# Three planes of expert three's gate and up matrices loaded ahead of the expert loop, and g_final loaded behind it

## The chip, the cores and the metric

One NeuronCore of a Trainium2 chip runs the whole kernel in one launch. The metric is the device time of one execution in microseconds (us). The engines of the core are PE (matmuls), DVE (vector), ACT (scalar), POOL and SP; SP computes nothing here and only issues loads. All transfers run on the core's 16 DMA engines.

## The reference

One step of a one-layer encoder: 512 prompt tokens and 32 sample tokens of width 1024. Two attention branches, merged by gates, then a mixture of experts, then a per-layer embedding gate and a last norm. The expert part is what matters here:

```
h = rmsnorm(x, g_ffn)
group = argmax(h @ w_group + b_group)                       # 4 groups of 8 experts
two experts of that group by top_k(softmax(h @ w_router))   # weights: softmax of both
for each block of rows of an expert e (32 experts):
    out = (silu(rows @ w_gate[e]) * (rows @ w_up[e])) @ w_down[e]    # 1024 -> 512 -> 1024
x = x + weighted sum of each token's two rows
x = x + sigmoid(rmsnorm(x, g_ple) @ w_ple_gate) * (p @ w_ple)
y = rmsnorm(x, g_final)
```

All is float32. An expert's three matrices are 2 MB each, 6 MB together, and all 32 experts are read once.

## The kernel before, in words

The front part (attention, merge, output projection) runs on PE until about 450 us. Then the rows are normed, stored to a DRAM tensor `normed_rows` (by ACT, semaphore `xn_stored` for the four prompt tiles), routed, and a table of rows for each expert is made on PE and DVE. Every expert has a block of 64 rows; an expert with more gets extra blocks after the loop. The 32 experts are worked off in 16 pairs. For a pair POOL gathers 128 rows by an indirect DMA (`xs_in`, three places), PE transposes them, DVE scales them (`xsT`); then for each of the two experts PE makes the gate and up products (`gate_up`, semaphore `gu_done`), ACT the silu, DVE the product, PE transposes it and makes the down product (`down`, `dn_done`), ACT copies the result out and POOL scatters it to a DRAM tensor `expert_rows` (`ye_stored`).

SBUF has places for the gate and up matrices of three experts (`w_gu[0..2]`, 32 KB in each partition, `gu_in[k]`), and four for down matrices. A matrix 1024 x 512 lies as 8 planes of 512 columns in each partition. `load_gu(k, e)` loads both matrices of expert `e` into place `k`; `load_planes(e, n, lo, hi)` loads planes `lo` to `hi` of one matrix, n = 0 for gate, 1 for up. Expert 3 uses place 0 again, after expert 0.

All weight loads are issued by SP, in the order in which they are written, on one hardware queue; SP's waits are what holds a load back. The order before the loop: expert 0 whole; the down matrix of expert 2; two quarters of expert 3's down matrix (`load_dn_over_rows`, each over a tile of rows that is done with); planes of expert 2; a third quarter; the down matrix of expert 1 and its gate planes; the first four planes of its up matrix; then, behind the wait for the first gather of rows (`xs_in[0]`, line 674), what is left of experts 1 and 2. From expert 3 on each gate and up load waits until PE has finished the same products of the expert three before (`next_gate_up` waits for `gu_done` at `e - 2`), and each down load until `dn_done` is at `e - 2`.

Behind the loop SP loads the inputs of the embedding gate, half of `w_ple_gate`, and `x_nat` from `normed_rows`; then it waits for the last expert and for all scatters (`ye_stored`), and loads for each tile the expert rows of its tokens (`yg`, in the order 0, 4, 1, 2, 3), with the other half of `w_ple_gate` behind the second.

The constants (router weights and biases, `g_fin`, sinks, gains) are loaded near the start on the semaphore `consts_in`; their readers wait for `16 * CONSTS`, lines 829, 1682 and 2055. `g_fin` holds `g_final` in all partitions, 4 KB in each. It is read in the last norms (`finish`) and by `keep_busy`, PE's filler matmuls at about 459 to 466 us, whose result nobody reads. Router tiles (`rt_...`) lie at 65 to 69.25 KB of the arena; `at(kb, dims)` gives the place at `kb` KB. The exponentials of the router are ACT's, released by `rt_exp_in`.

Of the kernel before, what the change touches and what calls it, by code (L numbers as in the profile page):

```python
# [32 lines left out]
P = 128  # L33
D = 1024
KD = D // P
# [22 lines left out]
GROUPS, PER = 4, 8  # L58
# [17 lines left out]
assert BODIES * BODY == PAIRS - 1 and 2 * BODY % PLACES == 0  # L76
CONSTS = 8
SLICES = 4
# [150 lines left out]
def _program(nc, A, ctx):  # L229
# [158 lines left out]

    work, keep = (65, 69.25), (130.25, 131.25)
    x_turned = [hb[:, 4 * D:5 * D].rearrange("p (c t) -> p c t", c=KD), xf[:, 4, :].rearrange("p (c t) -> p c t", c=KD),  # L390
# [11 lines left out]
    place_hot = rt(work, [2, 2, BLK])  # L402
    rt_thr, rt_step, rt_cnt = rt(work, [PER]), rt(work, [OVER]), rt(work, [EXPERTS])
    rt_cmp = rt(work, [EXPERTS, PER])
    rt_over = rt(work, [1])
    picks = at(69.25, [TILES, EXPERTS], BF16)
# [3 lines left out]
    w_dn = [[at(114.25, [4, D])], [hb[:, 0:4 * D].rearrange("p (c n) -> p c n", c=4)], [at(70.5, [2, D]), at(131.25, [2, D])]]  # L410
    w_dn.append([x_nat[:, c:c + 1, :] for c in range(4)])

    def dn_place(e):
# [140 lines left out]
    def _(sp):  # L554
# [28 lines left out]
        load(b_rt[:, GROUPS:], A['b_router'].to_broadcast([P, EXPERTS]), consts_in)  # L583
        load(g_fin[:, :], A['g_final'].unsqueeze(0).to_broadcast([P, D]), consts_in)
        load(sink_in[:, :], A['attn_sink'].to_broadcast([P, HEADS]), consts_in)
# [73 lines left out]
        load_dn_over_rows(0)  # L659
        load_dn_over_rows(1)  # L660
        sp.wait_ge(rows_full, 4)
        load_planes(2, 0, 0, 2)
# [9 lines left out]
        load_planes(1, 1, 2, 4)  # L672
        sp.wait_ge(rows_full, TILES)
        sp.wait_ge(xs_in[0], 16)
        load_planes(2, 1, 5, 8)
        load_planes(1, 1, 4, 6)
        load_planes(1, 1, 6, 8)
        for c in range(2, KD, 2):
            load_planes(2, 0, c, c + 2)
        load_planes(2, 1, 0, 1)  # L680
        load_planes(2, 1, 3, 5)
        load_dn_over_rows(3)

        def next_gate_up(k, e):
# [9 lines left out]
        LOOP = 2 * BODY  # L694
        for e in range(PLACES, PLACES + LOOP):
            next_gate_up(e % PLACES, e)
            if e > PLACES:
                next_down(dn_place(e), e)
        with sp.Fori(0, BODIES - 2) as i:
# [24 lines left out]
        sp.wait_ge(xn_stored, 16 * 4)  # L724
        load(x_nat[:, 0:4, :], xn_d[0:NP].rearrange("(t p) n -> p t n", p=P), x_in[0])

        sp.wait_ge(dn_done, EXPERTS)
# [195 lines left out]
    def _(pe):  # L923
# [427 lines left out]
        def keep_busy(n):  # L1351
            for _ in range(n):
                pe.matmul(ps[:, 2, :], ident[:, :], g_fin[:, 0:512], start=True, stop=True)

# [4 lines left out]
        def rows_turned(k, lo=0, hi=KD):  # L1359
# [4 lines left out]
            return mm  # L1364

        def expert_columns(k, m, c, g):

            return w_gu[k][:, m, c, :].rearrange("p m (q g j) -> p m q g j", g=2, j=2)[:, :, :, g, :]

        def gate_up(s, k, col):  # L1370
            for c in range(KD):
                for g in range(2):
                    mm = pe.matmul(ps[g * BLK:(g + 1) * BLK, 2 + s, :], xsT[:, c, col:col + BLK],  # L1373
                                   expert_columns(k, slice(0, 2), c, g), start=c == 0, stop=c == KD - 1)
            return mm
# [26 lines left out]
        def pair(i, body, j):  # L1402

            p = i * BODY + (body * BODY + j)
            for s in range(2):
                e = 2 * (body * BODY + j) + s
                k, use, d = e % PLACES, i * (2 * BODY // PLACES) + (e // PLACES + 1), dn_place(e)
                if s == 0:
                    pe.wait_ge(xsT_ready, p + 1)
                pe.wait_ge(gu_in[k], use * 32 + (32 * SLICES - 32 if k else 0))  # L1410
                gate_up(s, k, s * BLK).then_inc(gu_done, 1)
                if s == 0:
                    pe.wait_ge(xs_in[(j + 1) % 3], i * 16 + 16 * ((body * BODY + j + 1) // 3 + 1))
                    rows_turned((j + 1) % 3).then_inc(xsT_full, 1)
                pe.wait_ge(hid_ready, p * 2 + (s + 1))
                turn_hidden(s).then_inc(hidT_full, 1)
                pe.wait_ge(hidT_ready, p * 2 + (s + 1))
                pe.wait_ge(dn_in[d], i * (2 * BODY // PLACES * 16 * len(w_dn[d])) + dn_use(e) * 16 * len(w_dn[d]))
                pe.wait_ge(ye_free, p * 2 + (s + 1))
                down(s, d).then_inc(dn_done, 1)  # L1420
# [14 lines left out]
        half_of_expert(k, 0, 0, 1, 0).then_inc(gate_done, 1)  # L1435
        pe.wait_ge(gu_in[k], use * 32 + (32 * SLICES - 32 if k else 0) - 16)
        half_of_expert(k, 0, 1, 2, 256).then_inc(gu_done, 1)
# [10 lines left out]
        half_of_expert(k, 1, 0, 0, 0).then_inc(gate_done, 1)  # L1448
        pe.wait_ge(gu_in[k], use * 32 + (32 * SLICES - 32 if k else 0) - 16)
        half_of_expert(k, 1, 1, 3, 256).then_inc(gu_done, 1)  # L1450
# [493 lines left out]
    def _(dve):  # L1944
# [566 lines left out]
        def finish(i):  # L2511
            t = LAST_ORDER[i]
            r = ROWS[t]
            dve.wait_ge(x4_squares, i + 1)
            v = rstd(r, i)
# [63 lines left out]
```

## Time and profile before

| | us |
|---|---|
| median of three executions | 1022.1 (1021.7 to 1022.69) |
| the profiled execution | 1020.0 |
| its span, first to last instruction | 1017.9 |
| mean granted TensorE clock | 0.98 |
| PE busy | 911.9 (90%) |
| TensorE weight loads busy | 585.0 (57%) |
| DVE, ACT, POOL busy | 379.0, 258.3, 141.3 |
| chain that ended last: PE, DMA, DVE | 61%, 29%, 4% |
| of it, the load of up matrices | 26% |
| read from HBM, written | 256.09 MB, 16.85 MB |

The chain of waits is followed back from the last instruction: at each step to what released it, or to the instruction before it on its engine. A time to landing is that from the issue of a DMA until its semaphore has the last of 16 increments. All times below are microseconds from the span's start. "SPq" marks SP's instruction queue; L556 is the helper through which SP issues every load.

### The profile page before, as it was taken

The page shows a single profiled execution, that of the slowest core. Times are in us where ns is not written, and L with a number is a line of the kernel's source. Part 1 is how long each engine was busy: PE and PEld are TensorE (multiplying, and loading weights), DVE is VectorE, ACT ScalarE, POOL GpSimd, SP SyncE. Part 2 cuts the span into 40 slices and gives each one's busy share as a digit, 9 for nine tenths or more (in the row PEclk, how much of TensorE's full clock was granted, in tenths as well). Part 3 has the DMA queues.
Part 4 walks back from the last instruction along what each step waited for, and adds up shares of the span by engine and source line. Part 5 has one row for each costly group of instructions (what it writes and reads, how often), then busy time and mean ns, then how long its engine had stood idle before and what let it go on. Part 6 is the DMA issues. An engine that isn't in the chain of part 4 may idle for free.

```text
span 1017.9 us, 14245 instructions
## 1 busy us (share of the span) xinstructions
PE 911.9 (90%) x5747; PEld 585.0 (57%) x5750; DVE 379.0 (37%) x973; ACT 258.3 (25%) x525; POOL 141.3 (14%) x146
## 2 busy tenths in 40 slices
PE   7999999989999999989999988788887787888996
PEld 7969995557999997973333322222232222334775
DVE  4279998754233354362111110100110101113696
ACT  6354328664231342231000000000000000002542
POOL 2705432122110000001111101001101011000000
PEclk9999999999999999998999999999999999999998
DMA  8860602005734406487999999999999999997601
GB/s 268 115 162 1 208 1 63 1 2 164 220 77 110 119 2 269 150 311 298 423 423 428 426 429 425 426 427 426 427 425 427 426 427 427 428 422 317 259 22 68
DMA packets 61096, 265.88 MB, mean 261 GB/s; under 512 B 11118, under 2 KB 36094, under 8 KB 47312
## 3 DMA queue, kind: packets, MB, share of 16 engines
q1 hardware_dynamic: 55120, 253.08, 65.1%
q0 software_dynamic: 5296, 9.79, 2.7%
q10 hardware_dynamic: 624, 2.23, 0.6%
q8 instruction: 39, 0.64, 0.3%
q14 instruction: 17, 0.14, 0.0%
HBM read 256.09 MB, written 16.85 MB: 268 GB/s over the span
## 4 chain that ended last, share of the span: by engine, by line
PE 61%; DMA 29%; DVE 4%; issue 3%; ACT 2%; SPq 1%; POOL 0%; DVEq 0%; POOLq 0%; ACTq 0%
DMA arena<-in_w_up 26%; PE ps L1205 14%; PE ps L1373 12%; PE ps L1060 5%; PE ps L1238 4%; PE ps L1526 4%; PE ps L1398 4%; PE ps L1006 3%; PE ps L981 2%; PE ps L1150 2%; PE ps L1129 1%; PE ps L1099 1%; PE ps L943 1%; PE ps L1267 1%; PE ps L936 1%
## 5 line engine op out<-in xcount | busy, mean ns | idle before, releaser
L1373 PE MATMUL ps<-arena,hT 128*64 128x512 f32 x960 | 231.7, 635 | 37.9 <-DMA arena<-in_w_up 37.8
L1373 PEld LDWEIGHTS ps<-arena,hT 128*64 128x64 f32 x960 | 70.1, 139 | 196.6 <-issue 146.9
L2342 DVE TENSOR_TENSOR xf<-xf,ps 128x256 f32<-128x256 f32 x32 | 13.5, 421 | 398.1 <-ACT xf L1819 375.5
L1205 PE MATMUL ps<-arena_merge,arena_merge 128*128 128x256 f32 x624 | 99.7, 287 | 0.0
L891 POOL DMA_INDIRECT expert_rows<-xf,arena x32 | 32.0, 1001 | 422.9 <-ACT xf L1823 396.9
L1398 PE MATMUL ps<-arena,xf 128*64 128x512 f32 x336 | 76.7, 597 | 14.8 <-DVE xf L2345 13.4
L1205 PEld LDWEIGHTS ps<-arena_merge,arena_merge 128*128 128x128 f32 x624 | 87.5, 188 | 0.0
L1205 PE MATMUL ps<-xf_merge,arena_merge 128*128 128x256 f32 x480 | 82.0, 288 | 0.0
L1819 ACT ACTIVATE xf<-ps 128x256 f32<-128x256 f32 x30 | 11.5, 384 | 255.0 <-PE ps L1373 255.0
L1205 PEld LDWEIGHTS ps<-xf_merge,arena_merge 128*128 128x128 f32 x480 | 69.3, 188 | 0.0
L1823 ACT ACTIVATE xf<-ps 128x512 f32<-128x512 f32 x30 | 17.9, 597 | 160.9 <-PE ps L1398 160.9
L1398 PEld LDWEIGHTS ps<-arena,xf 128*64 128x64 f32 x336 | 25.7, 136 | 51.3 <-issue 48.5
L1238 PE MATMUL ps<-arena_merge,arena_merge 128*128 128x256 f32 x304 | 49.0, 286 | 1.2 <-DVE arena_merge L2176 1.0
L1526 PE MATMUL ps<-arena_gate,arena_gate 128*128 128x512 f32 x192 | 44.3, 391 | 1.3 <-DVE arena_gate L2484 0.8
L1238 PEld LDWEIGHTS ps<-arena_merge,arena_merge 128*128 128x128 f32 x304 | 42.9, 191 | 2.5 <-DVE arena_merge L2176 2.0
L2176 DVE TENSOR_TENSOR arena_merge<-arena,arena_merge 128x256 fp32r<-128x256 f32 (+2 forms) x34 | 39.9, 1226 | 9.0 <-ACT arena_merge L1590 9.0
L1060 PE MATMUL ps<-xf_merge,arena_front 128*128 128x272 f32 x256 | 43.2, 289 | 0.0
L1590 ACT ACTIVATE arena_merge<-arena 128x256 fp32r<-128x256 f32 (+3 forms) x43 | 37.1, 919 | 21.3 <-DMA arena<-in_w_branch_a 10.4
L1398 PE MATMUL ps<-hT,xf 128*64 128x512 f32 x160 | 36.5, 598 | 5.2 <-DVE xf L2345 5.2
L1526 PEld LDWEIGHTS ps<-arena_gate,arena_gate 128*128 128x128 f32 x192 | 35.8, 188 | 9.2 <-ACT arena L1861 1.0
L1060 PEld LDWEIGHTS ps<-xf_merge,arena_front 128*128 128x128 f32 x256 | 36.2, 189 | 0.2
L1687 ACT ACTIVATE arena<-arena,stat 128x257 f32<-128x257 f32 (+7 forms) x57 | 29.6, 520 | 4.0 <-DVE stat L2094 4.0
(323 smaller groups left out, 1306.2 us busy)
## 6 DMA issues: line engine op xcount, KB each, us to landing
arena<-in_w_gate SPq DMA_DIRECT2D x30, 2048.0 KB, 30.5
arena<-in_w_up SPq DMA_DIRECT2D x30, 2048.0 KB, 37.3
arena<-in_w_down SPq DMA_DIRECT2D x11, 2048.0 KB, 36.0
arena<-in_w_down SPq DMA_DIRECT2D x20, 1024.0 KB, 30.9
hT<-in_w_down SPq DMA_DIRECT2D x10, 2048.0 KB, 36.5
arena<-in_w_in SPq DMA_DIRECT2D x10, 1024.0 KB, 6.5
arena<-in_w_in SPq DMA_DIRECT2D x3, 2048.0 KB, 11.1
arena<-in_w_gate SPq DMA_DIRECT2D x8, 512.0 KB, 9.0
```

Source lines behind the costliest of these rows:

```text
L891: pool.indirect_dma_start(ys, bass.IndirectOffsetOnAxis(ap=of, axis=0), src, None, bounds_check=row_bound, oob_is_err=False).then_inc(s, 16)
L981: mm = pe.matmul(w[:, a * 512:a * 512 + HALF], rounded(st, "front"), rounded(mv[:, c, a * HALF:(a + 1) * HALF]), start=c == 0 and k == 0, ...
L1006: mm = pe.matmul(ps[0:ROWS[t], 6 + slot, 0:256], rounded(st[:, c, tok(t)]), rounded(mv[:, c, :], "front"), start=c == 0 and k == 0, stop=c ...
L1060: mm = pe.matmul(w[:, a * 512:a * 512 + HALF], rounded(st, "front"), rounded(mv[:, c, a * HALF:(a + 1) * HALF]), start=c == 0 and k == 0, ...
L1205: mm = pe.matmul(w[:, 2 * lo_t:lo_t + hi_t], rounded(st[:, c, cols]), rounded(mv[:, c, lo_t:hi_t]), start=c == 0 and k == 0, stop=c == pla ...
L1238: mm = pe.matmul(w[:, q * QW:(q + 1) * QW], rounded(st[t // 2][:, t % 2, m, :]), rounded(mv[:, m, :]), start=m == 0 and k == 0, stop=m == ...
L1373: mm = pe.matmul(ps[g * BLK:(g + 1) * BLK, 2 + s, :], xsT[:, c, col:col + BLK], expert_columns(k, slice(0, 2), c, g), start=c == 0, stop=c ...
L1398: mm = pe.matmul(ps[g * BLK:(g + 1) * BLK, 6 + s, :], hidT[s][:, c % 2, c // 2 * BLK:(c // 2 + 1) * BLK], dn_at(k, c)[:, g * 512:(g + 1) * ...
L1526: mm = pe.matmul(w[:, cols], rounded(st[:, c, :], "gate"), rounded(mv[:, c, cols], "gate"), start=c == 0 and k == 0, stop=c == KD - 1 and ...
L1590: return act.activation(rounded(dst, stage), src, ACT.Copy)
L1687: act.activation(v, v, ACT.Exp, bias=stat[:, 0, g, j:j + 1], scale=-1.0, accum_out=stat[:, 1, g, j:j + 1]).then_inc(exp_done, 1)
L2176: return dve.tensor_tensor(rounded(v, stage), v, rounded(hi, stage).bitcast(F32), ALU.subtract)
```

## The change

The matrices of expert 3 are loaded in two parts. Planes 0, 1 and 2 of its gate and up matrices get rooms of their own, 4 KB in each partition: room 0 is the tile `g_fin`, room 1 lies at 64.5 to 68.5 KB of the arena, room 2 in two pieces at 68.5 and at 112 KB. Room 0 is loaded behind the second quarter of expert 3's down matrix, rooms 1 and 2 behind the fourth quarter and a wait for `rt_exp_in`. All six loads count on `gu_in[0]`, and a wait for expert 0's two loads stands ahead of the first. Planes 3 to 7 are loaded, as before, when PE has finished expert 0's products. PE reads the rooms in the first pass of the loop's first body alone, for expert 3; every wait on `gu_in[0]` from expert 3 on is higher by 96.

Three loads of 512 KB, planes 4 to 7 of expert 1's up matrix and planes 2 and 3 of expert 2's gate matrix, move from behind the wait for the first gather to ahead of it, behind a new wait for `xn_stored`.

`g_fin` is loaded behind `x_nat` near the end, as `CONSTS` is now 7, and DVE waits for it before the first `finish`. `keep_busy` reads the identity matrix four times over in its place. Some router tiles move to 78.5 to 80 KB.

```diff
--- before.py
+++ after.py
@@ -74,7 +74,7 @@
 BODY = 3
 BODIES = (PAIRS - 1) // BODY
 assert BODIES * BODY == PAIRS - 1 and 2 * BODY % PLACES == 0
-CONSTS = 8
+CONSTS = 7
 SLICES = 4
 
 
@@ -386,7 +386,7 @@
         assert rt_at[lo] <= int(hi * 256)
         return at(first / 256, dims, dt)
 
-    work, keep = (65, 69.25), (130.25, 131.25)
+    work, keep, late = (65, 69.25), (130.25, 131.25), (78.5, 80)
     x_turned = [hb[:, 4 * D:5 * D].rearrange("p (c t) -> p c t", c=KD), xf[:, 4, :].rearrange("p (c t) -> p c t", c=KD),
                 at(78.5, [KD, NS])]
     turned_in = {0: x_turned[0], 1: x_turned[0], 2: x_turned[1], 3: x_turned[0], 4: x_turned[2]}
@@ -400,15 +400,27 @@
     rt_el, rt_t1, rt_t2 = rt(work, [EXPERTS + 8]), rt(work, [EXPERTS + 8]), rt(work, [EXPERTS + 8])
     rt_free, rt_pen = rt(work, [8 + GROUPS]), rt(work, [GROUPS])
     place_hot = rt(work, [2, 2, BLK])
-    rt_thr, rt_step, rt_cnt = rt(work, [PER]), rt(work, [OVER]), rt(work, [EXPERTS])
-    rt_cmp = rt(work, [EXPERTS, PER])
-    rt_over = rt(work, [1])
+    rt_cmp = rt(late, [EXPERTS, PER])
+    rt_thr, rt_step, rt_cnt = rt(late, [PER]), rt(late, [OVER]), rt(late, [EXPERTS])
+    rt_over = rt(late, [1])
     picks = at(69.25, [TILES, EXPERTS], BF16)
     rt_ti = at(69.75, [EXPERTS]).bitcast(I32)
 
     w_gu = [at(32.5, [2, KD, DE]), at(0, [2, KD, DE]), at(80, [2, KD, DE])]
     w_dn = [[at(114.25, [4, D])], [hb[:, 0:4 * D].rearrange("p (c n) -> p c n", c=4)], [at(70.5, [2, D]), at(131.25, [2, D])]]
     w_dn.append([x_nat[:, c:c + 1, :] for c in range(4)])
+
+    def apart(kb, step):
+
+        v = at(kb, [DE])
+        return bass.AP(tensor=v.tensor, offset=v.offset, ap=[v.ap[0], [int(step * 256), 2], [1, DE]])
+
+    ROOMS = [g_fin[:, :].rearrange("p (m n) -> p m n", m=2), at(64.5, [2, DE]), apart(68.5, 112 - 68.5)]
+    ROOM_LOADS = 2 * len(ROOMS)
+
+    def gu_count(e, k, use):
+
+        return use * 32 + (32 * SLICES - 32 if k else 16 * ROOM_LOADS if e >= PLACES else 0)
 
     def dn_place(e):
 
@@ -581,7 +593,6 @@
         load(w_rt[:, :, GROUPS:], A['w_router'][0].rearrange("(p c) n -> p c n", c=KD), consts_in)
         load(b_rt[:, 0:GROUPS], A['b_group'].to_broadcast([P, GROUPS]), consts_in)
         load(b_rt[:, GROUPS:], A['b_router'].to_broadcast([P, EXPERTS]), consts_in)
-        load(g_fin[:, :], A['g_final'].unsqueeze(0).to_broadcast([P, D]), consts_in)
         load(sink_in[:, :], A['attn_sink'].to_broadcast([P, HEADS]), consts_in)
         load_gain(1, consts_in)
         load_gain(2, consts_in)
@@ -658,6 +669,14 @@
 
         load_dn_over_rows(0)
         load_dn_over_rows(1)
+
+        def load_room(c):
+
+            for m in range(2):
+                load(ROOMS[c][:, m], A[('w_gate', 'w_up')[m]][0, PLACES].rearrange("(p c) n -> p c n", c=KD)[:, c], gu_in[0])
+
+        sp.wait_ge(gu_in[0], 32)
+        load_room(0)
         sp.wait_ge(rows_full, 4)
         load_planes(2, 0, 0, 2)
         load_planes(2, 1, 1, 3)
@@ -671,15 +690,20 @@
         load_planes(1, 1, 0, 2)
         load_planes(1, 1, 2, 4)
         sp.wait_ge(rows_full, TILES)
+        sp.wait_ge(xn_stored, 16 * 4)
+        load_planes(1, 1, 4, 6)
+        load_planes(1, 1, 6, 8)
+        load_planes(2, 0, 2, 4)
         sp.wait_ge(xs_in[0], 16)
         load_planes(2, 1, 5, 8)
-        load_planes(1, 1, 4, 6)
-        load_planes(1, 1, 6, 8)
-        for c in range(2, KD, 2):
+        for c in range(4, KD, 2):
             load_planes(2, 0, c, c + 2)
         load_planes(2, 1, 0, 1)
         load_planes(2, 1, 3, 5)
         load_dn_over_rows(3)
+        sp.wait_ge(rt_exp_in, 1)
+        load_room(1)
+        load_room(2)
 
         def next_gate_up(k, e):
 
@@ -692,10 +716,13 @@
             load_dn(k, e)
 
         LOOP = 2 * BODY
-        for e in range(PLACES, PLACES + LOOP):
+        sp.wait_ge(gu_done, 1)
+        for m in range(2):
+            load(w_gu[0][:, m, len(ROOMS):], A[('w_gate', 'w_up')[m]][0, PLACES].rearrange(
+                "(p c) n -> p c n", c=KD)[:, len(ROOMS):], gu_in[0])
+        for e in range(PLACES + 1, PLACES + LOOP):
             next_gate_up(e % PLACES, e)
-            if e > PLACES:
-                next_down(dn_place(e), e)
+            next_down(dn_place(e), e)
         with sp.Fori(0, BODIES - 2) as i:
             for e in range(PLACES + LOOP, PLACES + 2 * LOOP):
                 next_gate_up(e % PLACES, i * LOOP + e)
@@ -723,6 +750,7 @@
         load(w_pg[:, 0:KD // 2], w_pg_d[:, 0:KD // 2], w_pg_in[0])
         sp.wait_ge(xn_stored, 16 * 4)
         load(x_nat[:, 0:4, :], xn_d[0:NP].rearrange("(t p) n -> p t n", p=P), x_in[0])
+        load(g_fin[:, :], A['g_final'].unsqueeze(0).to_broadcast([P, D]), consts_in)
 
         sp.wait_ge(dn_done, EXPERTS)
         sp.wait_ge(slots_ready, 1)
@@ -1350,7 +1378,7 @@
 
         def keep_busy(n):
             for _ in range(n):
-                pe.matmul(ps[:, 2, :], ident[:, :], g_fin[:, 0:512], start=True, stop=True)
+                pe.matmul(ps[:, 2, :], ident[:, :], ident[:, :].unsqueeze(1).to_broadcast([P, 4, P]), start=True, stop=True)
 
         keep_busy(3)
         pe.wait_ge(index_ready, 3)
@@ -1363,15 +1391,20 @@
                 mm = pe.transpose(w[:, c, :], xs[k][:, c:D:KD], ident[:, :])
             return mm
 
+        def every_other(w, g):
+
+            return w.rearrange("p m (q g j) -> p m q g j", g=2, j=2)[:, :, :, g, :]
+
         def expert_columns(k, m, c, g):
 
-            return w_gu[k][:, m, c, :].rearrange("p m (q g j) -> p m q g j", g=2, j=2)[:, :, :, g, :]
-
-        def gate_up(s, k, col):
+            return every_other(w_gu[k][:, m, c, :], g)
+
+        def gate_up(s, k, col, rooms=[]):
             for c in range(KD):
                 for g in range(2):
                     mm = pe.matmul(ps[g * BLK:(g + 1) * BLK, 2 + s, :], xsT[:, c, col:col + BLK],
-                                   expert_columns(k, slice(0, 2), c, g), start=c == 0, stop=c == KD - 1)
+                                   every_other(rooms[c], g) if c < len(rooms) else expert_columns(k, slice(0, 2), c, g),
+                                   start=c == 0, stop=c == KD - 1)
             return mm
 
         def half_of_expert(k, s, m, bank, col):
@@ -1407,8 +1440,8 @@
                 k, use, d = e % PLACES, i * (2 * BODY // PLACES) + (e // PLACES + 1), dn_place(e)
                 if s == 0:
                     pe.wait_ge(xsT_ready, p + 1)
-                pe.wait_ge(gu_in[k], use * 32 + (32 * SLICES - 32 if k else 0))
-                gate_up(s, k, s * BLK).then_inc(gu_done, 1)
+                pe.wait_ge(gu_in[k], gu_count(e, k, use))
+                gate_up(s, k, s * BLK, ROOMS if body == 0 and e == PLACES else []).then_inc(gu_done, 1)
                 if s == 0:
                     pe.wait_ge(xs_in[(j + 1) % 3], i * 16 + 16 * ((body * BODY + j + 1) // 3 + 1))
                     rows_turned((j + 1) % 3).then_inc(xsT_full, 1)
@@ -1433,7 +1466,7 @@
         pe.wait_ge(xsT_ready, p + 1)
         pe.wait_ge(gate_in[0], 16)
         half_of_expert(k, 0, 0, 1, 0).then_inc(gate_done, 1)
-        pe.wait_ge(gu_in[k], use * 32 + (32 * SLICES - 32 if k else 0) - 16)
+        pe.wait_ge(gu_in[k], gu_count(EXPERTS - 2, k, use) - 16)
         half_of_expert(k, 0, 1, 2, 256).then_inc(gu_done, 1)
         pe.wait_ge(hid_ready, p * 2 + 1)
         turn_hidden(0).then_inc(hidT_full, 1)
@@ -1446,7 +1479,7 @@
         k, use = (EXPERTS - 1) % PLACES, (EXPERTS - 1) // PLACES + 1
         pe.wait_ge(gate_in[1], 16)
         half_of_expert(k, 1, 0, 0, 0).then_inc(gate_done, 1)
-        pe.wait_ge(gu_in[k], use * 32 + (32 * SLICES - 32 if k else 0) - 16)
+        pe.wait_ge(gu_in[k], gu_count(EXPERTS - 1, k, use) - 16)
         half_of_expert(k, 1, 1, 3, 256).then_inc(gu_done, 1)
         pe.wait_ge(rows_in, 32 + 32)
         for c in range(2):
@@ -2511,6 +2544,8 @@
         def finish(i):
             t = LAST_ORDER[i]
             r = ROWS[t]
+            if i == 0:
+                dve.wait_ge(consts_in, 16 * (CONSTS + 1))
             dve.wait_ge(x4_squares, i + 1)
             v = rstd(r, i)
             dve.scalar_tensor_tensor(yo[t][0:r, :], x_nat[0:r, t, :], v, g_fin[0:r, :], ALU.mult, ALU.mult)\
```

## Rows read from the trace of the kernel before

**Rows 1.** The page, second part: busy tenths in 40 slices of the span.
```profile
DMA  8860602005734406487999999999999999997601
```

**Rows 2.** Stretches: length, each engine's busy us (instructions), PE clock, DMA share, GB/s.
```profile
core 0: us, PE busy (x) PEld busy (x) DVE busy (x) ACT busy (x) POOL busy (x), PEclk, DMA share, GB/s
456.60:462.00 5.40, 4.32 (x18) 2.46 (x19) 3.38 (x20) 1.60 (x3) 1.46 (x2) 0.50 0.01 5
...
490.00:580.00 90.00, 83.17 (x384) 30.56 (x382) 9.55 (x18) 6.87 (x14) 11.11 (x11) 1.00 1.01 425
580.00:900.00 320.00, 259.79 (x1124) 89.78 (x1122) 28.23 (x50) 20.23 (x41) 30.22 (x30) 0.97 1.01 427
...
936.00:942.00 6.00, 5.46 (x24) 4.50 (x25) 3.41 (x3) 3.10 (x3) 0.52 (x1) 1.00 0.27 105
```

**Rows 3.** Waits of PE, 460 to 920 us: total us, times, longest us.
```profile
PE ps L1373 <- DMA arena<-in_w_up: 37.8, 20, 3.3
```

**Rows 4.** The chain of waits, whole span: start, us, what.
```profile
460.24 4.52 DMA xf<-normed_rows,arena
464.89 0.69 PE ps L1363 x4
465.61 1.30 DVE hT L2374 x2
466.95 7.42 PE ps L1373 x32
...
577.90 35.69 DMA arena<-in_w_up
```

**Rows 5.** Timeline of SP's issues: start, us, instruction.
```profile
474.42 0.33 SPq L556 DMA_DIRECT2D arena<-in_w_gate  x1
474.79 0.43 SPq L556 DMA_DIRECT2D arena<-in_w_up  x1
487.24 0.33 SPq L556 DMA_DIRECT2D arena<-in_w_gate  x1
487.61 0.43 SPq L556 DMA_DIRECT2D arena<-in_w_up  x1
...
500.05 0.33 SPq L556 DMA_DIRECT2D arena<-in_w_gate  x1
```

**Rows 6.** DMA issues, the one at 474.79: size, us to landing.
```profile
arena<-in_w_up SPq DMA_DIRECT2D x1, 2048.0 KB, 16.7
```

**Rows 7.** ACT's store of the last rows: timeline, and DMA issues.
```profile
454.28 0.33 ACTq L1780 DMA_DIRECT2D normed_rows<-xf  x1
...
normed_rows<-xf ACTq DMA_DIRECT2D x1, 512.0 KB, 3.6
```

**Rows 8.** SP's issues at 382 us, queue empty, and their us to landing.
```profile
382.27 0.35 SPq L556 DMA_DIRECT2D arena<-in_w_gate  x1
382.67 0.43 SPq L556 DMA_DIRECT2D arena<-in_w_up  x1
...
arena<-in_w_gate SPq DMA_DIRECT2D x1, 2048.0 KB, 8.3
...
arena<-in_w_up SPq DMA_DIRECT2D x1, 2048.0 KB, 12.8
```

**Rows 9.** Stretches around room 0's issue, columns as in rows 2.
```profile
426.00:431.00 5.00, 5.00 (x44) 5.00 (x44) 1.30 (x9) 1.02 (x1) 0.00 (x0) 1.00 0.25 69
436.00:438.00 2.00, 2.00 (x19) 2.00 (x19) 1.79 (x14) 1.22 (x2) 0.00 (x0) 1.00 0.07 23
```

**Rows 10.** DMA issues, the one at 487.61: size, us to landing.
```profile
arena<-in_w_up SPq DMA_DIRECT2D x1, 2048.0 KB, 14.4
```

**Rows 11.** DMA issues, a 512 KB load at 429.01: us to landing.
```profile
x_nat<-in_w_down SPq DMA_DIRECT2D x1, 512.0 KB, 3.8
```

**Rows 12.** POOL's gather of rows issued at 495.04: us to landing.
```profile
DMA to landing us min/median/max: 13.5/13.5/13.5
```

**Rows 13.** DMA issues, `g_fin` at 24.64: us to landing.
```profile
g_fin<-in_g_final SPq DMA_DIRECT2D x1, 512.0 KB, 3.7
```

**Rows 14.** SP's issue of `x_nat`: timeline, and us to landing.
```profile
917.74 3.11 SPq L556 DMA_DIRECT2D x_nat<-normed_rows  x1
...
x_nat<-normed_rows SPq DMA_DIRECT2D x1, 2048.0 KB, 25.5
```

**Rows 15.** The chain of waits behind the loop: start, us, what.
```profile
941.31 5.18 DMA arena<-expert_rows
946.59 1.30 DVE x_nat L2466
```

## The prediction

> **What bounds the kernel now.** I read the page's DMA line first [rows 1]: from the twentieth of 40 slices (about 483 us) to the thirty-sixth the 16 DMA engines are full. The stretches say it more sharply [rows 2]: between 456.6 and 462 us they are idle (share 0.01), between 490 and 580 us full at 425 GB/s, between 580 and 900 us full at 427 GB/s. PE's waits in the expert loop are nearly all for a weight load, 37.8 us in 20 waits [rows 3]. In the chain [rows 4] a load is first the late step at 577.90 us: up to there PE sets the pace (one expert in some 12.8 us), from there on the DMA stream does. The reader is to take from this that the end follows the time at which this unbroken stream gets through its bytes, and that bytes moved out of it count only if the stream can then really run earlier.
>
> What lets it run is the queue's own waits [rows 5]. The loads of expert 3 go out at 474.42, of expert 4 at 487.24, of expert 5 at 500.05: each as PE has finished the gate and up products of the expert that held the place (`gu_done`). That is PE's clock, not the DMA's. So the question of this change is how late the stream is when expert 4's loads are issued. Expert 3's up matrix, issued at 474.79, lands 16.7 us later, 491.5 [rows 6]: 4.3 us after the issue of expert 4's. This is all the backlog there is at that moment.
>
> **The change part by part.**
>
> *Bytes taken out of the stream.* (a) Three loads of 512 KB (planes 4 to 7 of expert one's up, 2 and 3 of expert two's gate) move from behind the wait for the first gather to behind `xn_stored`. The last store of rows is issued at 454.28 and lands 3.6 us later, 457.9 [rows 7], so they run in the idle gap. (b) Room 0 of expert three, 512 KB, goes out behind the load at 429.01; its wait for `gu_in[0]` was over when expert zero's up landed, 382.67 + 12.8 = 395.5 [rows 8], so nothing is held up behind it. The DMAs are a quarter busy from 426 to 431 and nearly idle from 436 to 438 [rows 9], so its 1.2 us (524 KB at 425 GB/s) are hidden; were that cover gone it would push the loads behind it 1.2 us, and those have until 466 us. (c) Rooms 1 and 2, 1024 KB, are only moved ahead of 474.42, into a time when the stream is full in any case: nothing. The four extra issues on SP at some 0.4 us each are done by about 472, before SP's next wait ends at 474.42 [rows 5]: nothing. Together 2048 KB leave the stream ahead of expert 4. One such load lands behind the other 382.67 + 12.8 less 382.27 + 8.3, 4.9 us [rows 8].
>
> *How much of it counts.* With 4.9 us less in front, expert 3's last piece would land at 491.5 - 4.9 = 486.6, ahead of the issue at 487.24, which no edit moves forward. The queue runs dry and has to start again from empty. What that costs is in the trace: at 382.67 an up matrix was issued behind a gate matrix with the queue empty, as expert 4's would be now, and landed after 12.8 us [rows 8]. So expert 4's up would land at 487.61 + 12.8 = 500.4; before it landed at 487.61 + 14.4 = 502.0 [rows 10]. The gain is 1.6 us, not 4.9. Bounds: 4.3 (all of the backlog, if the start from empty cost nothing) and 0 (if the DMA engine that is last at 900 us is one that had caught up at 487 us already; the spread of the engines is not in a view). I take 1.6, from the row that has the same two loads in the same order. From 490 us on the queue never empties again, and this gain lasts to the end of the stream.
>
> Beside that row stands a rule of the Trainium skill, "DMA: Bandwidth & Descriptors", section "Anatomy of one DMA": a fixed cost of about 2.0 us and bytes at 436 GB/s. The trace has 8.3 less 4.9, 3.4 us, for a 2048 KB load from empty. By the rule the up matrix would land at 498.9 and the step would be worth an estimated 3 us; the row decides the sum, and the rule's result is the second rival below.
>
> *The gather's delay.* The three loads share the DMAs with the first gather of rows, which is on the chain: issued at 460.24, landed 4.52 us later, then PE's transposes, DVE, and expert 0 at 466.95 [rows 4]. In the trace of before nothing else runs there. A 512 KB load issued on a quiet queue lands after 3.8 us [rows 11]; two more and the gather itself, 524 KB each at 425 GB/s, make 457.9 + 3.8 + 3.7 = 465.4 for the last of the four, 0.6 us behind the 464.8 of before. Everything PE does shifts by this, the issue of expert 4's loads too, so it is lost in full. Bounds: 0 (the gather gets through between the loads) and 9.0, since a gather in the full loop takes 13.5 us and not 4.5 [rows 12]. I take 0.6: at 460.24 the queue holds three short loads, no loop of them.
>
> *The tail.* `g_fin`, 512 KB, leaves the constants at 24.64 us, where nothing on the chain waits for it (it took 3.7 us there [rows 13]; PE is busy with projections), so taking it out is worth nothing: its first reader is the last norm. It comes back behind the load of `x_nat`, which is issued at 917.74 and lands 25.5 us later, 943.2 [rows 14]. That is later than the issue of the first gathered output rows at 941.31 on the same queue, and those are on the chain: they land 5.18 us on, and DVE starts at 946.59 [rows 15]. So at least one DMA engine now has 1.2 us more before it can turn to them. On the average the DMAs are only 0.27 busy between 936 and 942 us [rows 2], so the other engines swallow it. Bounds 0 and 1.2; I take 0.9, nearer to the slowest engine, because a landing is that of the last of the 16. The wait for `g_fin` on DVE itself costs nothing: it stands before the first norm of an output, more than 30 us after that load.
>
> *Nothing else.* PE's clock filler reads the identity matrix in place of `g_fin`, 512 columns as before, in a time when PE waits for the gather. The moved router tiles change addresses, no instruction. The gate and up products of expert 3 read three planes from other places, same shapes, and those are there 30 us ahead.
>
> Sum: -1.6 + 0.6 + 0.9 = -0.1 us on the profiled execution's 1020.0 us (span 1017.9, and 2.1 us around it): 1019.9. The median of the runs shown is 1022.1, 2.1 us above that execution; the same difference on it gives 1022.0.
>
> **The rivals.**
>
> *The prefetch counts for more.* If the stream is not dry at 487.24, or restarts at once, the step is worth up to the whole backlog, 4.3 us: -4.3 + 0.6 + 0.9 = -2.8, 1019.3. For it: the engines end at different times, and the last one may carry work across. Against it: 4.9 us are taken from a backlog of 4.3, and the row from empty. By the skill's fixed cost (section named above) it would be an estimated -1.5, 1020.6.
>
> *The gather waits behind weights (slower).* Place: 457.9 to 465 us. If the packets of the gather come behind those of the three loads as they do in the loop, its landing moves by up to 9.0 us and PE's whole schedule with it: the DMAs then simply stay dry for longer, as every later issue hangs on PE. Price at that bound: -1.6 + 9.0 + 0.9 = +8.3, 1030.4. It turns the result slower, by over 2 us, from a delay of 2.7 us on. For it: 13.5 against 4.5 us [rows 4, 12]. Against it: the loads hold 1536 KB, 3.7 us of work, of which over half is done when the gather's first packets could come.
> Here the Trainium skill, "DMA: Bandwidth & Descriptors", section "Queues, rings and completion order", speaks against the change: each DMA engine takes turns between its queue rows a whole packet at a time. By it the gather waits out a started packet at every turn, which no row of this gap shows; it is what would lead to this rival's delay, and its price is that from the rows above.
>
> *The prefetch is worth nothing.* The engine that ends last had no backlog at 487 us: 0 + 0.6 + 0.9 = +1.5, 1023.6.
>
> **How the numbers follow.** A difference of 0.2% (2 us) is about what a measurement tells from none. Forecast (-0.1, between -1.6 and +1.6 as the parts of it vary): 0.64. Nothing gained: 0.07. Both are within 0.2%, 0.71. The prefetch for more: 0.16, faster. The gather behind weights: 0.13, slower. The range reaches down to the first rival's 1019.3 and up to 1024.6, the last rival's 1023.6 with 1 us more of delay; most of the slow rival's long tail is left out.
>
> **What would show it.** DMA share above 0.5 between 459 and 462 us; the first gather's landing at 465.4 and expert 0's products at 467.5 in place of 466.95; between 485 and 489.5 us a dip in the DMA share that was not there; PE's first wait for a load a little later than at 577.9; the last down matrix about 1 us earlier; between 935 and 947 us some of it given back, with the first output rows landing 6 us after their issue. The prediction is wrong if there is no dip at 487 us, if the gather takes over 7 us, or if the end moves by more than 2 us either way.

## The result, and the profile after

The changed kernel takes 1024.86 us (median of 20 executions, 1022.65 to 1028.72), the kernel before 1021.78 (20 executions, 1019.68 to 1024.16): ratio 1.0029, 95% interval 1.0021 to 1.0037, slower by 3 us. The prediction was 1022.0, with a range from 1019.3 to 1024.6 and a chance of 0.13 for slower. Three single executions further below took 1810, 3115 and 5000 us and are left out of the ratios.

The profiled execution has a span of 1022.4 us against 1017.9, 4.5 us more. Where it arises can be read off the chain of waits (start, us, what), compared step by step with [rows 4, 15]:

```profile
462.31 5.20 DMA xf<-normed_rows,arena
467.64 0.70 PE ps L1391 x4
...
469.71 7.42 PE ps L1405 x32
...
580.65 35.88 DMA arena<-in_w_up
...
938.24 5.95 DMA expert_rows<-xf,arena
944.26 6.75 DMA arena<-expert_rows
951.11 1.30 DVE x_nat L2499
```

The gather is issued 2.07 us later (462.31 for 460.24) and takes 5.20 for 4.52; expert 0's products start at 469.71 for 466.95, 2.76 later. The output rows' load is issued at 944.26 for 941.31, 2.95 later, and takes 6.75 for 5.18, so DVE starts 4.52 later, which is the end's shift. So there are three large steps and a small one: 2.07 ahead of the gather, 0.68 in it, 0.2 over the whole loop, 1.57 in the tail.

The first is in code that the change hardly touches. In the stretches (length, busy us and instructions of each engine, PE clock, DMA share, GB/s) the changed kernel has PE at 1.2 GHz for 3.4 us where before had 2.4 GHz throughout (granted clock 0.57 and 1.00); the first fence is the changed kernel, the second the kernel before:

```profile
386.00:390.00 4.00, 3.95 (x19) 3.75 (x20) 2.66 (x3) 0.34 (x1) 0.00 (x0) 0.57 1.01 430
```
```profile
386.00:390.00 4.00, 3.92 (x30) 3.73 (x31) 2.85 (x3) 0.52 (x1) 0.00 (x0) 1.00 0.99 418
```

19 matmuls in 4 us and not 30: the rest of that work comes some 1.5 us later (an estimate: 11 matmuls at 4/30 us each). From 382 to 386 us PE is busy for 2.88 us in the changed kernel and for 2.90 in the one before, so what it did ahead of the stretch does not tell the two apart. Nor does the program decide it: e5 below is the changed kernel once more, and its profile has no such stretch. What is left of the 2.07 us has no cause in these views.

What the stream of weights does at expert 4's issue:

```profile
477.18 0.33 SPq L568 DMA_DIRECT2D arena<-in_w_gate  x1
477.55 0.43 SPq L568 DMA_DIRECT2D arena<-in_w_up  x1
490.00 0.33 SPq L568 DMA_DIRECT2D arena<-in_w_gate  x1
490.37 0.43 SPq L568 DMA_DIRECT2D arena<-in_w_up  x1
```
```profile
484.00:487.00 3.00, 3.00 (x16) 0.90 (x14) 0.00 (x0) 0.00 (x0) 1.04 (x1) 1.00 0.97 401
487.00:490.00 3.00, 2.95 (x14) 0.69 (x10) 0.00 (x0) 0.00 (x0) 0.00 (x0) 1.00 0.21 83
490.00:492.00 2.00, 0.59 (x4) 0.40 (x6) 0.99 (x3) 0.38 (x1) 0.00 (x0) 1.00 0.72 131
492.00:580.00 88.00, 81.69 (x373) 29.22 (x373) 9.46 (x16) 6.48 (x13) 11.13 (x11) 1.00 1.00 425
580.00:900.00 320.00, 260.61 (x1124) 92.65 (x1124) 29.05 (x52) 20.59 (x42) 30.23 (x30) 0.96 1.01 427
```
```profile
arena<-in_w_up SPq DMA_DIRECT2D x1, 2048.0 KB, 13.2
```

The timeline of SP, the stretches, and the time to landing of the up matrix issued at 490.37. The queue runs dry: the DMA share is 0.21 between 487 and 490, where before had 1.05. The matrix lands 13.2 us after its issue and not 14.4 [rows 10]; so at this point the stream is 1.2 us nearer to PE than before, where 12.8 and so 1.6 had been forecast. From 492 us on the DMA share and the rate are those of before [rows 2], and of the 1.2 us nothing is left at the end of the loop.

### The profile page after: what moved, and what is told of

It reads as the page before. It is cut to its first block, busy times and chain, and to the rows that moved or that the text cites. A ratio compares the mean times of both kernels' runs of the same rounds, so it can differ in the third digit from the quotient of the medians.

```text
span 1022.4 us, 14251 instructions
## 1 busy us (share of the span) xinstructions
PE 915.9 (90%) x5750; PEld 589.2 (58%) x5750; DVE 378.7 (37%) x973; ACT 258.2 (25%) x525; POOL 141.3 (14%) x146
## 4 chain that ended last, share of the span: by engine, by line
PE 60%; DMA 29%; DVE 5%; issue 3%; ACT 2%; SPq 0%; POOL 0%; DVEq 0%; POOLq 0%; ACTq 0%
DMA arena<-in_w_up 26%; PE ps L1233 13%; PE ps L1405 12%; PE ps L1088 5%; PE ps L1266 5%; PE ps L1559 4%; PE ps L1431 4%; PE ps L1034 3%; PE ps L1009 2%; PE ps L1178 2%; PE ps L1157 1%; PE ps L1127 1%; PE ps L1295 1%; PE ps L971 1%; PE ps L964 1%
## 5 line engine op out<-in xcount | busy, mean ns | idle before, releaser
L832 POOL TENSOR_TENSOR arena_front<-arena,arena_front 128x512 fp32r<-128x512 f32 (+1 forms) x17 | 24.8, 1491 | 42.6 <-ACT arena_front L1623 42.4
```

Source lines behind the costliest of these rows:

```text
L832: return pool.tensor_tensor(rounded(v, stage), v, rounded(hi, stage).bitcast(F32), ALU.subtract)
```

## The experiments

Theory A, formed on the two traces: the prefetched bytes bring nothing, since each of the 16 DMA engines starts expert 4 from empty, and the one that ends the loop last was one with no backlog before; the gather's delay and `g_fin`'s load are both paid in full; the rest is chance. Rival B: something that I had put at nothing (moved router tiles, the filler, the clock) costs 1 to 2 us, and the prefetch's 1.2 us are real.

The first four kernels are compared with the same runs of before, the next four with a second set, the last three with a third. The ratio stated can differ from that of the medians by up to 0.1%, and with some ten runs of a kernel its interval is some 0.1% wide to either side, about 1 us.

**e1, `g_fin` late alone.** On the kernel before:
```diff
-CONSTS = 8
+CONSTS = 7
-        load(g_fin[:, :], ..., consts_in)            # among the constants
         load(x_nat[:, 0:4, :], xn_d[0:NP]..., x_in[0])
+        load(g_fin[:, :], ..., consts_in)
# and the filler on ident, the wait in finish, as in the change
```


> The kernel before with only g_fin's load moved behind x_nat (and the filler reading the identity). Theory A (the tail pays for g_fin on the DMA engine that is last): the first output rows land some 6.7 us after their issue and not 5.2, the whole is slower by 1.2 to 1.8 us, ratio 1.0012 to 1.0018. Rival B (the quiet DMAs swallow it, the 4.5 us between the profiles came from earlier): within 0.5 us of before, 5.2 us to landing.

Measured: 1023.46 against 1022.03, ratio 1.0014 (1.0005 to 1.0023), 1.4 us slower. Its chain has the longer landing, 6.38 us for 5.18 [rows 15], a little less than the 6.7 expected:
```profile
937.69 6.01 DMA expert_rows<-xf,arena
943.78 6.38 DMA arena<-expert_rows
```
The tail's step stands alone; B's "swallowed" is out.

**e2, the three loads early alone.** On the kernel before:
```diff
         sp.wait_ge(rows_full, TILES)
+        sp.wait_ge(xn_stored, 16 * 4)
+        load_planes(1, 1, 4, 6); load_planes(1, 1, 6, 8); load_planes(2, 0, 2, 4)
         sp.wait_ge(xs_in[0], 16)
         load_planes(2, 1, 5, 8)
-        load_planes(1, 1, 4, 6); load_planes(1, 1, 6, 8)
-        for c in range(2, KD, 2):
+        for c in range(4, KD, 2):
```


> The kernel before with only the three 512 KB loads moved ahead of the wait for the first gather. Theory A (the stream runs dry at expert 4's issue and starts from empty for every DMA engine, so nothing of the 3.7 us is kept, and the gather's delay is lost in full): first gather 5.1 to 5.3 us to landing, slower by 0.5 to 1 us. Rival B (1.2 us of the prefetch last to the end): faster by about 0.5 us. Either way the up matrix of expert 4 lands 12.8 to 13.3 us after its issue, not 14.4.

Measured: 1023.09 against 1022.03, ratio 1.0011 (0.9999 to 1.0023). The interval touches 1, so the time alone leaves slower just short of shown; a gain of 0.5 us is outside it. Chain and stretches:
```profile
461.69 5.16 DMA xf<-normed_rows,arena
```
```profile
456.60:462.00 5.40, 2.96 (x16) 1.98 (x17) 4.12 (x27) 1.09 (x4) 0.31 (x1) 0.50 0.56 189
...
487.00:490.00 3.00, 2.31 (x12) 0.44 (x8) 0.23 (x1) 0.38 (x1) 0.00 (x0) 1.00 0.59 236
```
The gap of [rows 2] is filled (0.56 for 0.01), the gather pays 0.6 us for it, and the hole turns up again at 487 us (0.59). The up matrix of expert 4 lands 13.2 us after its issue, as expected.

**e3, the change with `g_fin` loaded later.**
```diff
         load(x_nat[:, 0:4, :], xn_d[0:NP]..., x_in[0])
-        load(g_fin[:, :], ..., consts_in)
         ...
                 load(w_pg[:, KD // 2:], w_pg_d[:, KD // 2:], w_pg_in[1])
+                load(g_fin[:, :], ..., consts_in)
```


> The changed kernel with g_fin loaded behind the first three loads of output rows' queue (behind the second half of w_ple_gate) and not ahead of them. Theory A: the first output rows land 5.2 us after their issue again, 1.2 to 1.8 us faster than the changed kernel, so before +1.3 to +1.8. Rival B (the tail is not the cause): still +3, though the landing may be 5.2.

Measured: 1022.73 against 1022.03, ratio 1.0006 (0.9995 to 1.0017). The changed kernel's ratio was 1.0029 and 1.0030 (e5): some 2.4 us come back, more than forecast, though the intervals leave room for the forecast 1.2 to 1.8. The first output rows land after 5.74 us, better than the change's 6.75 but not the 5.2 expected. The span of this profile, 1022.1, is hardly below the change's 1022.4, as PE's clock fell ahead of expert 0 here (see e7).

**e4, the rooms alone.** e3 with the three loads back behind `xs_in[0]`.

> As e3, and the three 512 KB loads back behind the wait for the first gather: only the three rooms are left. Theory A (prefetched planes of expert 3 are worth nothing, the rest of the change costs nothing): same as before within 0.5 us, first gather 4.5 us to landing. Rival B (the change costs something else, in the router tiles or in the clock around 386 us): still slower by 1 to 2 us. Rival C (the planes are worth their bytes): 1 to 2 us faster.

Measured: 1022.38 against 1022.03, ratio 0.9999 (0.9987 to 1.0011): no difference, with some 1.2 us of doubt to either side. Of the rooms only room 0, 512 KB or 1.2 us, leaves the stream here; it brings nothing, and the moved router tiles, the filler on the identity and the higher counts cost nothing that shows. The interval alone leaves B and C of that expectation their lower edges, 1 us; the loop of its profile is 0.1 us shorter than before (table below), which speaks against C.

**e5, the changed kernel again.**

> The changed kernel itself, run again beside the others. Theory A: 2.2 to 3 us slower than before (0.7 of the gather and 1.4 of g_fin's load, nothing gained), and the half clock stretch at 386 us that its first profile had and the profile of before had not is chance: this profile may well be without it, with the first gather issued at about 461 us. Rival B (the change causes that clock stretch): it is there again.

Measured: 1024.95 against 1021.74, ratio 1.003 (1.0017 to 1.0044). Stretch of its profile, same columns:
```profile
386.00:390.00 4.00, 3.90 (x30) 3.49 (x30) 3.10 (x4) 0.78 (x1) 0.00 (x0) 1.00 1.03 434
```
The same program, and no stretch at half clock at 386 us, so the change does not bring it about by itself. Two more of the later profiles have it (e7, e10), none of the three of kernels without rooms; whether the change makes it more frequent is not settled.

**e6, bytes added.** e4 with expert 3 loaded whole, and the rooms loaded late and unused:
```diff
-        sp.wait_ge(gu_in[0], 32)
-        load_room(0)                                  # the early one
         sp.wait_ge(rt_exp_in, 1)
+        load_room(0)
         load_room(1); load_room(2)                    # all on a semaphore room_in
-        # planes 3 to 7 of expert 3
+        next_gate_up(0, PLACES)                       # expert 3 whole
```


> As e4, but expert 3 is loaded whole and the three rooms (1536 KB, 3.7 us of DMA) are loaded late, behind the other loads, and read by nobody: bytes added ahead of expert 4 instead of taken out. Theory A (the DMA engine that ends last is just short of dry when expert 4's loads are issued, so bytes more cost all and bytes less bring nothing): 3 to 3.7 us slower than before. Rival B (this stretch has slack either way): within 1 us. Rival C (bytes count both ways, the gain was lost elsewhere): 3.7 us slower as well, and then e4 must have lost 1.2 us somewhere.

Measured: 1025.26 against 1021.74, ratio 1.0036 (1.0023 to 1.0049): 3.5 to 3.7 us slower for 3.7 us of DMA. Its up matrix of expert 4, issued at 487.06, lands 18.8 us later, for 14.4 before:
```profile
arena<-in_w_up SPq DMA_DIRECT2D x1, 2048.0 KB, 18.8
```
Bytes more at this place cost at least what they take (the loop of its profile is even 4.8 us longer), bytes less (e4, e2) bring nothing: the kernel before stood at the edge where its queue just fails to run dry.

**e7, the rooms for expert 4.** On e3. Expert 4's loads are the first that PE holds back at a dry queue; its planes leave the stream behind that point.
```diff
-   load(ROOMS[c][:, m], ...[0, PLACES]...[:, c], gu_in[0])
+   load(ROOMS[c][:, m], ...[0, PLACES + 1]...[:, c], room_in)
-        sp.wait_ge(gu_done, 1)                        # planes 3 to 7 of expert 3
+        next_gate_up(0, PLACES)                       # expert 3 whole
+        sp.wait_ge(gu_done, 2)                        # planes 3 to 7 of expert 4
# PE reads the rooms at e == PLACES + 1, behind a wait for room_in
```


> The rooms are given to expert 4 in place of expert 3 (own semaphore; expert 3 loaded whole; g_fin as in e3; the three 512 KB loads early). Bytes now leave the stream behind the issue of expert 4's loads. Theory A: 3.7 us less to load behind it, some 1.3 us of it lost as the queue is nearly dry at that issue, 0.7 lost by the gather: 1.5 to 3 us faster than before. Rival B (planes held in rooms are worth nothing wherever they belong): 0.5 to 1 us slower, as e3.

Measured: 1021.35 against 1021.74, ratio 0.9988 (0.9975 to 1.0002). The interval touches 1; B, slower by 0.5 to 1 us, is outside it, but the gain is smaller than forecast. The stretches of this kernel:
```profile
487.00:490.00 3.00, 3.00 (x16) 0.96 (x14) 0.00 (x0) 0.00 (x0) 0.00 (x0) 1.00 0.97 382
490.00:493.00 3.00, 2.06 (x10) 0.59 (x6) 0.42 (x1) 0.38 (x1) 0.00 (x0) 1.00 0.67 214
```
and PE's timeline:
```profile
461.20 4.78 PE L1383 MATMUL ps<-ident 128*128 128x512 f32 x6
467.91 1.46 PE L1393 MATMUL ps<-ident,xf 128*128 128x128 f32 x8 [1.94 <-DMA xf<-normed_rows,arena]
469.16 1.92 PE L1383 MATMUL ps<-ident 128*128 128x512 f32 x2
471.01 7.88 PE L1407 MATMUL ps<-arena,hT 128*64 128x512 f32 x32
```
The queue is short again at expert 4's issue (0.67 from 490 to 493 us). That costs nothing that shows: from expert 0's first product to the last scatter this kernel takes 465.5 us, and e9 below, whose queue is not short, 465.4. What is lost lies ahead of expert 0. The gather takes 5.41 us, and PE, idle for 1.94 us ahead of its landing, does the filler behind it at half clock (1.92 us for the 1.02 of most profiles), so expert 0 starts 3.2 us behind the landing (471.01 less 467.78), before 2.2 us [rows 4]. The profile of e3 has the same, 3.6 us. These two are among the five profiles with all three loads early; of the other eight none has it.

**e8, as e7 with the three loads back behind the gather.**

> As e7 with the three 512 KB loads back behind the wait for the first gather. Theory A: the stream ahead of expert 4 is 2.5 us longer, behind it 3.7 us shorter, nothing lost by the gather: 1 to 1.5 us faster than before. Rival B: the same as before.

Measured: 1020.43 against 1021.74, ratio 0.9979 (0.9967 to 0.9991). Faster, by 1.3 us in the medians and 2.1 by the ratio; rival B of e8 is out, and with e9 that of e7.

**e9 and e10, two loads early, and one.** On e8; the other stay behind the gather.
```diff
+        sp.wait_ge(xn_stored, 16 * 4)
+        load_planes(1, 1, 4, 6)
+        load_planes(1, 1, 6, 8)                       # e9 alone
         sp.wait_ge(xs_in[0], 16)
```


> As e8 (rooms for expert 4, g_fin last) with two of the three 512 KB loads ahead of the first gather: the stream ahead of expert 4's issue is as long as before, behind it 3.7 us shorter. Theory A: 3 to 3.5 us faster than before, less 0.2 to 0.5 for the gather. Rival B (each early load costs the gather its own time, whatever the number): as e8, 1.3 to 2 us faster.

> As e9 with one load early. Theory A: the stream ahead is 1.2 us longer, the gather is not touched: 2 to 2.5 us faster than before. Rival B: no faster than e8.

Measured: e9 1018.62, ratio 0.9964 (0.9951 to 0.9977); e10 1019.4, ratio 0.9973 (0.9963 to 0.9983), both against 1021.99. e9 has the lowest median of this study, 3.4 us below before (3.7 by the ratio, 2.3 to 5.0 by the interval) and some 6 below the change, from eight executions between 1016.3 and 1022.0. Its lead over e10 is within the intervals. The queue is not short around expert 4's issue at 492 us (share 1.06 from 490 to 493, 1.00 from 490 to 498), and the gather keeps nearly its time (4.52 before, 5.20 in the change):
```profile
490.00:493.00 3.00, 2.06 (x10) 0.57 (x6) 0.42 (x1) 0.39 (x1) 0.00 (x0) 1.00 1.06 450
```
```profile
464.56 4.76 DMA xf<-normed_rows,arena
...
936.95 5.95 DMA expert_rows<-xf,arena
942.97 5.45 DMA arena<-expert_rows
```

**e11, a fourth filler.** e9 with `keep_busy(4)`.

> As e9 with four filler matmuls ahead of the gather's landing and not three. Profiles with a late gather had PE idle for 1.7 to 2.4 us before the transposes, and two of them then a stretch at half clock over expert 0. Theory A (idle time, and so the half clock, is filled): 0 to 0.5 us faster than e9, no half clock stretch begins between 465 and 472 us. Rival B (the filler itself becomes late at half clock): 0.3 to 0.6 us slower than e9.

Measured: 1018.95 against 1021.99, ratio 0.9973 (0.9961 to 0.9985). Its interval and that of e9 overlap in most of their width: no difference that these runs can tell. Neither profile has half clock over the start of expert 0, so there was nothing for the fourth filler to mend; whether it would is not settled.

A table that takes the chance of the front out, from the profiled executions, all in us. It has the first gather's landing (start plus duration), expert 0's first product, the time from there to POOL's last scatter (this is the loop), and from that scatter to the span's end. The last two columns go into the landing of a late load, expert 30's up matrix. Its semaphore gets 16 increments, which I take for one from each DMA engine, and their mean and the last of them are given from expert 0's first product on.

| kernel | gather landed | expert 0 | loop | to the end | increments, mean | last |
|---|---|---|---|---|---|---|
| before | 464.8 | 467.0 | 468.3 | 82.6 | 434.3 | 441.5 |
| e1 `g_fin` late | 466.8 | 469.0 | 468.7 | 83.9 | 434.4 | 441.9 |
| the change | 467.5 | 469.7 | 468.5 | 84.2 | 433.5 | 441.7 |
| e5 the change again | 466.0 | 468.2 | 468.5 | 83.8 | 433.7 | 441.7 |
| e2 loads early | 466.9 | 469.1 | 468.4 | 83.1 | 433.6 | 441.5 |
| e3 `g_fin` last | 466.7 | 470.4 | 468.5 | 83.2 | 433.9 | 441.7 |
| e4 rooms of expert 3 | 466.4 | 468.6 | 468.2 | 82.7 | 433.6 | 441.4 |
| e6 bytes added | 464.2 | 466.4 | 473.1 | 82.9 | 438.1 | 446.3 |
| e8 rooms of expert 4, loads late | 465.3 | 467.5 | 467.2 | 82.7 | 433.2 | 440.5 |
| e10 one load early | 467.2 | 469.4 | 465.7 | 82.7 | 432.0 | 438.9 |
| e9 two loads early | 469.3 | 471.5 | 465.4 | 82.9 | 431.6 | 438.6 |
| e7 three loads early | 467.8 | 471.0 | 465.5 | 82.8 | 431.7 | 438.7 |
| e11 fourth filler | 465.2 | 467.4 | 465.9 | 83.3 | 431.4 | 439.1 |

The loop is the same within 0.5 us in the seven profiles in which no byte of expert 4 or later was taken out of the stream and none added (before, e1 to e5 and the change), whatever left it ahead of expert 4, and it moves as soon as bytes leave behind that point. The increments show how the gain is lost: in the five of these with bytes taken out their mean comes 0.4 to 0.8 us earlier than before, and the last does not (0.1 earlier to 0.2 later). In e7, e9 and e10 mean and last both come 2.3 to 2.9 us earlier. The column to the end has `g_fin`'s price: 83.8 to 84.2 in the three profiles with it ahead of the output rows, 82.6 to 83.3 in the ten others, about 1.1 us in the means.

## Why the prediction was wrong

Most of the mechanism was right: the stream runs dry at expert 4's issue, the gather pays for the loads beside it, the tail pays for `g_fin`. Of its three signs of being wrong, two did not show: the dip at 487 us is there, and the gather took 5.2 us and not over 7. The third did, as the end moved by 3 us. The sum was wrong mainly by one term, the gain.

- **How much of it counts: the step that failed.** "I take 1.6, from the row that has the same two loads in the same order", and "this gain lasts to the end of the stream". The up matrix did land 1.2 us nearer to its issue (13.2 for 14.4; 13.6 in e4), but no kernel kept any of that: the loop takes 468.2 to 468.7 us with and without, and the lone rooms (e4) have a ratio of 0.9999. A landing is that of the last of 16 increments. The prediction named the case in which such a gain is worth nothing, as its lower bound of 0 and as the third rival (0.07): the engine that is last 400 us later had no backlog at 487 us. The increments of expert 30's up matrix bear this out, as their mean gained 0.4 to 0.8 us and the last of them nothing, and e6 shows the edge from its other side. That it is one certain engine throughout is argued, as the trace does not say whose an increment is. I should have priced this term at its lower bound.
- **The estimate by a rule, 3 us.** It did not hold either. The Trainium skill, "DMA: Bandwidth & Descriptors", section "Anatomy of one DMA", gives its fixed cost of about 2.0 us for the gpsimd path, and SP's loads are not on that path. By it the up matrix would have landed 11.3 us after its issue (498.9 less 487.61); it took 13.2.
- **The tail.** Forecast 0.9. The runs of e1 give 1.4 (0.5 to 2.4), the landings of the first output rows about 1.1: 6.3 to 6.8 us in the three profiles with `g_fin` ahead of them, 5.2 to 5.8 in the ten without. The 1.57 of the first two profiles was partly luck, as before has one of the shortest of these landings. So the price was near the upper bound of 1.2, and "the other engines swallow it" did not help; but this term was not far off.
- **The gather's delay.** Forecast 0.6, measured 0.68, and 0.64 in e2: right. What I did not price is what PE does in the longer wait. In e3 and e7, where it had been idle for 2.15 and 1.94 us, it then worked at 1.2 GHz for a part of the way to expert 0 (granted clock 0.63 from 466 to 470 us in e3, 0.59 from 468 to 471 us in e7), and expert 0 started 1.4 and 1.0 us late. This adds to the loss in some executions; in the change (idle for 1.75 us) and e2 (2.42 us) it did not happen. How often it does, the runs can't tell.
- **Rooms 1 and 2, room 0, the router tiles, the filler, early `g_fin`: nothing.** Right, within e4's interval.
- **The slow rival.** Slower, as it said, but not by its mechanism: the gather never took more than 5.4 us. The true case was the third rival's, with the tail at its upper end: 0 + 0.7 + 1.1 to 1.4 = 1.8 to 2.1 us, against 3.1 measured (2.1 to 3.8 by the interval), and 2.5 as the sum of e1 and e2. The remaining 0.5 to 1.3 us is not settled; the clock ahead of expert 0 is the one candidate that a profile shows.
- **The chances.** The case that came true had 0.07, though the only ground for preferring 1.6 was one landing. The range was not too narrow for the parts that are known: with 0.7 and 1.4 the third rival comes to 1024.2, inside its end of 1024.6. The measured 1024.86 is past it by the part that stays open.

The question with which the prediction began, how late the stream is at expert 4's issue, held the answer to what would work: planes that leave the stream ahead of a point at which PE holds a dry queue are worth nothing, planes behind it are worth most of their bytes. The change gave its rooms to expert 3, the last before that point. Given to expert 4 (e9), with two loads moved into the idle gap to make up for rooms 1 and 2 in the full stretch ahead of that point, they shorten the loop by 2.9 of their 3.7 us, and the whole by 3.4 in the medians. Without any load moved (e8) the loop gains 1.1, with one (e10) 2.7, with three (e7) 2.8: no more than with two, and the gather pays.

## What to carry to other kernels

Before moving loads ahead, find the first later load whose issue hangs on the consumer and not on the queue. Where the queue is already nearly dry at that point, bytes taken out ahead of it only make a hole there; take out bytes behind it, and ahead of it just as many as the prefetch itself adds there. Price a gain seen in one landing at zero unless the last of the 16 increments keeps it to the end of the stream, and a cost seen in one landing in full. This rests on one kernel.

## What the runs showed of the hardware that I had not expected

Single executions of one program lie 2 to 6 us apart (1022.65 to 1028.72 for the change), and part of that is where stretches of some 3.4 us at 1.2 GHz fall: one at 386 us costs an estimated 1.5 us and was there in one of two profiles of the same kernel. The first gather was issued between 459.8 and 464.6 us in thirteen profiles of kernels with nearly the same front. A comparison of two single profiles has to take such steps out before it explains anything.

The 16 increments of one load drift apart in a full stream: 2.8 us from first to last for expert 3's up matrix, 15.2 us for expert 30's, some 417 us later, in the kernel before.

A small transfer queued behind a large one, half a megabyte at a time when the DMAs were 0.27 busy on the average, cost 1.4 us (0.5 to 2.4).
